# The first shift vector of a transformer block: condition standing, weights moving in rows of 512

## The chip, the cores and the metric

One NeuronCore of one Trainium2 chip runs the whole program. The metric is the device time of one execution in microseconds (us). TensorE (PE) multiplies, and its sequencer loads the standing operand (PEld); VectorE (DVE), ScalarE (ACT) and GpSimd (POOL) work on tiles of 128 partitions; SyncE (SP) issues most of the transfers. Each engine runs its own list of instructions in order, and the lists meet only at semaphores.

## What is computed

A two-layer hybrid block on 256 latent tokens and 256 context tokens, 1024 channels, float32. Each sublayer starts with an RMS norm whose result is scaled and shifted by vectors that come from a condition, one for the latent and one for the context tokens:

```
s_lat = silu(c);  s_ctx = silu(c_ctx)
mod   = s_lat @ w_ada[l] + b_ada[l]          # 9 vectors of 1024: shift, scale, gate of three sublayers
mod_c = s_ctx @ w_ada[l] + b_ada[l]
h     = rmsnorm(s, g_norm) * (1 + scale) + shift
s     = s + 0.5 * gate * (silu(h @ w_g) * (h @ w_u)) @ w_out     # the first and the last sublayer
```

The change concerns the very first shift vector (1024 channels, two conditions) of layer 0.

## The kernel before, in words

Channels lie on partitions: `x` is [128, 8, 512], eight tiles of 128 channels by 512 tokens. Every product of the large layers is made of three products of rounded halves (high and low part of the weights and of the tokens, 128x512 each, lines 1548 to 1550). Weight blocks come through a ring of four buffers (`raw`); ScalarE makes the high part (`cast`, L637) and VectorE the low part (`lower`, L1049).

The opening, by engine, in the order of each list:

- SyncE loads `ada_first` in four parts of 2 MB (L420), in the order 0, 2, 1, 3. Parts 0 and 1 are the weights of the first shift vector, parts 2 and 3 those of the first scale vector. Then it loads the first four `raw` blocks (L426).
- ScalarE issues the load of x and the small vectors, makes `c_act` = silu of the two conditions, [128, 8, 2] (L624), and `c_wide`, the same values on all partitions (L631); then the square of the last tile of x (L652). It waits for the sums of squares, takes the root (L654), casts the first two weight blocks, and waits for the first scaled tile.
- GpSimd adds up the squares of the other seven tiles (L516 to L519).
- VectorE makes the first scale vector by itself: sixteen multiply-and-sum instructions over 1024 elements (L1491), eight tiles by two conditions. Then, in `norm`, the reciprocal of the root (L1024); then `modulations`, which waits for the shift vector (`s_adad` at 8) and for its own sums and adds the biases (L995, L1001, L1011); the low parts of two blocks (L1049); and then the scaled tiles (L1033).
- TensorE, in `norm`, waits for the constants and the squares, sums them over the partitions with eight small matmuls (L1534, L1535), then runs `first_modulation`: for each of eight tiles of the shift vector, eight matmuls whose standing operand is a 128x128 block of weights and whose moving operand is the two columns of `c_act`, 64 in all, into `mod_ps` (bank 7). Behind that it waits for the reciprocal and spreads it over the partitions (L1541), and then waits for the tiles of the norm for the first two blocks (`first_two`).

So `mod_ps` gets the shift vector with channels on partitions, as VectorE reads it. All later modulation vectors are made by VectorE during the feed-forward stages and are not touched.

The tile `ada_first` lies on a part of SBUF that the hidden tiles of the first feed-forward stage (`a_hi`, `a_lo`) use later. Banks 2 and 3 of PSUM are first used by the second pair of weight blocks.

Of the kernel before, what the change touches and what calls it, by code (L numbers as in the profile page):

```python
# [9 lines left out]
ACT = mybir.ActivationFunctionType  # L10
# [3 lines left out]
P = 128  # L14
D = 1024
KD = D // P
LAT, CTX = 256, 256
TOK = LAT + CTX
# [26 lines left out]
ADA_FIRST = 2 * KD  # L45
# [66 lines left out]
def build_program(nc, a):  # L112
    with ExitStack() as ctx:
        def sb(name, shape, dt=F32, at=ctx):
            return at.enter_context(nc.sbuf_tensor(name, shape, dt))

        def sem(name):
            return ctx.enter_context(nc.semaphore(name))
# [37 lines left out]
        c_act = sb("c_act", [P, KD, 2])  # L156
# [5 lines left out]
        ident = consts[:, C_ID:C_ID + P]  # L162
# [17 lines left out]

        with ExitStack() as s:
            ada_first = sb("ada_first", [P, ADA_FIRST, KD * P], at=s)
        with ExitStack() as s:
            a_hi = sb("a_hi", [P, KF, TOK], F32R, at=s)
            a_lo = sb("a_lo", [P, KF, TOK], F32R, at=s)
# [4 lines left out]
        s = ExitStack()  # L190
# [14 lines left out]
        s = ExitStack()  # L205
# [34 lines left out]
        ps = ctx.enter_context(nc.psum_tensor("ps", [P, 8, 512], F32))  # L240
        mod_ps = ps[:, 7, 0:2 * DEPTH * ADA].rearrange("p (t s) -> p t s", s=2)
# [4 lines left out]
        s_first = [sem(f"ada_first_loaded{i}") for i in range(4)]  # L246
# [5 lines left out]
        s_out = sem("out_stored")  # L252
        s_set = sem("set_up")
        s_cact = sem("c_act_ready")
        s_adad = sem("ada_tiles_done")
        s_adv = sem("ada_first_sums")
        s_adc = sem("ada_sums_kept")
        s_mods = sem("mods_ready")
# [116 lines left out]
        def halves(n):  # L375
            return [(i, slice(i * LAT, (i + 1) * LAT)) for i in range(n // LAT)]
# [33 lines left out]
        def mods_at(l, which):  # L410

            return ((1, 3, 3), (4, 5, 5))[l][which]
# [195 lines left out]
        def _(act):  # L608
# [26 lines left out]
            def cast(j, cols=KD * P):  # L635

                return act.activation(w_hi[:, j % RING, 0:cols], raw[:, j, 0:cols], ACT.Copy)  # L637

            def landed(j, base, it=0):

                act.wait_ge(s_raw[j], 16 * (base // RING + 1) + 16 * it)

            def norm(s, l, which, n):

                def casts(lo, hi):
                    for j in range(lo, hi):
                        landed(j, STAGE_BASE[s])
                        cast(j).then_inc(s_hi, 1)
                if 0 < s < 6:
                    casts(0, 2)  # L650
                act.wait_ge(*tile_ready(s, KD - 1))
                act.activation(buf_b[:, 1, 0:n], x[:, KD - 1, 0:n], ACT.Square).then_inc(s_sq, 1)  # L652
                act.wait_ge(s_sum, s + 1)
                act.activation(rms[:, 0:n // P], ps[:, 6, 0:n // P], ACT.Sqrt, bias=eps_col[:, 0:1],  # L654
                               scale=1.0 / D).then_inc(s_rt, 1)
                if s == 0:
                    casts(0, 2)
                if which < 3:
                    act.wait_ge(s_mods, mods_at(l, which))
                for k in range(KD):  # L660
                    act.wait_ge(s_t, KD * s + k + 1)
                    if which == 3:
                        act.activation(out_t[:, k, :], buf_a[:, k % 2, 0:n], ACT.Identity,
                                       scale=nfin[:, k:k + 1]).then_inc(s_fin, 1)
                        continue
                    if k >= 2:
                        act.wait_ge(s_h, KD * s + k - 1)
                    for i, cols in halves(n):
                        last = act.activation(buf_b[:, k % 2, cols], buf_a[:, k % 2, cols], ACT.Identity,  # L669
                                              bias=mod[:, l, 3 * which * KD + k, i:i + 1],  # L670
                                              scale=gain[:, l, which, k, i:i + 1])
                    link(last)
                    act.activation(h_hi[:, k, 0:n], buf_b[:, k % 2, 0:n], ACT.Copy).then_inc(s_hhi, 1)
                    if k == KD - 3 and s in FFN_STAGE:
                        casts(2, 4)
# [301 lines left out]
        def _(vec):  # L977
# [8 lines left out]
            def modulations(l, g0, g1):  # L986

                vec.wait_ge(s_const, 48)
                t0, t1 = g0 * KD, g1 * KD
                if g0 == 0 and l == 0:  # L990
                    vec.wait_ge(s_adad, KD)
                    src = mod_ps[:, 0:KD, :]
                    t1 = KD
                    vec.wait_ge(s_adv, 2 * KD)
                    vec.tensor_tensor(  # L995
                        mod[:, 0, KD:2 * KD, :], scale_first[:, :, :],
                        vecs[:, 0, KD:2 * KD].rearrange("p (t o) -> p t o", o=1).to_broadcast([P, KD, 2]), ALU.add)
                else:
                    r0 = (ADA * l + t0 - ADA_FIRST) // 2
                    src = mod_rest[:, r0:r0 + (t1 - t0) // 2, :].rearrange("p r (t s) -> p (r t) s", s=2)  # L1000
                link(vec.tensor_tensor(  # L1001
                    mod[:, l, t0:t1, :], src,
                    vecs[:, l, t0:t1].rearrange("p (t o) -> p t o", o=1).to_broadcast([P, t1 - t0, 2]), ALU.add))
                for which in range(3):
                    if g0 <= 3 * which + 2 < g1 and which != 1:
                        gate = mod[:, l, (3 * which + 2) * KD:(3 * which + 3) * KD, :]
                        link(vec.tensor_scalar(gate, gate, 0.5, None, ALU.mult))
                    if not g0 <= 3 * which + 1 < g1:
                        continue
                    g = V_N1 + which * KD  # L1010
                    link(vec.scalar_tensor_tensor(  # L1011
                        gain[:, l, which, :, :], mod[:, l, (3 * which + 1) * KD:(3 * which + 2) * KD, :], 1.0,
                        vecs[:, l, g:g + KD].rearrange("p (t o) -> p t o", o=1).to_broadcast([P, KD, 2]),
                        ALU.add, ALU.mult))
                vec.engine_nop().then_inc(s_mods, 1)
# [492 lines left out]

        @block.tensor
        def _(pe):  # L1510
            def ada_tile(t, w):

                for k in range(KD):
                    last = pe.matmul(mod_ps[:, t, :], w[:, k * P:(k + 1) * P], c_act[:, k, :],  # L1514
                                     start=(k == 0), stop=(k == KD - 1))
                last.then_inc(s_adad, 1)

            def first_modulation():

                pe.wait_ge(s_cact, 1)  # L1520
                for t in range(KD):
                    if t % (ADA_FIRST // 4) == 0:
                        pe.wait_ge(s_first[t // (ADA_FIRST // 4)], 16)
                    ada_tile(t, ada_first[:, t, :])

            def norm(s, n):
                if s == 0:
                    pe.wait_ge(s_set, 3)
                    pe.wait_ge(s_const, 48)
                pe.wait_ge(s_acc, s + 1)  # L1530
                pe.wait_ge(s_sq, s + 1)
                for t in range(n // P):
                    cols = slice(t * P, (t + 1) * P)
                    pe.matmul(ps[:, 6, t:t + 1], buf_a[:, 0, cols], ones[:, 0:1], start=True, stop=False)  # L1534
                    ins = pe.matmul(ps[:, 6, t:t + 1], buf_b[:, 1, cols], ones[:, 0:1], start=False, stop=True)  # L1535
                ins.then_inc(s_sum, 1)
                if s == 0:
                    first_modulation()
                pe.wait_ge(s_inv, s + 1)
                for t in range(n // P):  # L1540
                    ins = pe.matmul(ps[:, 6, t * P:(t + 1) * P], inv[:, t:t + 1].to_broadcast([P, P]), ident,  # L1541
                                    start=True, stop=True)
                ins.then_inc(s_bc, 1)
# [449 lines left out]
def lay_out(v):  # L1993

    v = {k: np.asarray(z) for k, z in v.items()}

    def blocks(w):

        return w.reshape(w.shape[0] // P, P, w.shape[1] // P, P).transpose(2, 1, 0, 3).reshape(w.shape[1] // P, P, -1)
# [5 lines left out]
    tok = np.concatenate([v["x"][0], v["ctx"].reshape(CTX, D)], 0)  # L2005
    out = {"xT": tok.T.reshape(KD, P, TOK).transpose(1, 0, 2)}
    out["cT"] = np.stack([v["c"][0], v["c_ctx"]], 1).reshape(KD, P, 2).transpose(1, 0, 2)
    out["w_ada"] = blocks(v["w_ada"][0][:, :KD * P])
    out["w_ada_t"] = v["w_ada"].transpose(0, 2, 1).reshape(DEPTH * ADA, P, D)[KD:]
    out["c_rows"] = np.stack([v["c"][0], v["c_ctx"]])  # L2010
    ups, downs = [], []
# [6 lines left out]
    proj, bas, gate, merge, outs, vec, pw, rows = [], [], [], [], [], [], [], []  # L2018
    for l in range(DEPTH):
        w = v["w_in"][l]  # L2020
# [41 lines left out]
```

## Time and profile before

| | |
|---|---|
| median of 3 runs | 2533.12 us (2524.01 to 2538.27) |
| the profiled execution | 2533.53 us, span of its instructions 2531.9 us |
| TensorE matmuls busy | 2419.6 us, 96% of the span, 13688 records |
| VectorE busy | 1396.8 us, 55% |
| ScalarE busy | 869.1 us, 34% |
| GpSimd busy | 219.6 us, 9% |
| mean granted clock of TensorE | 0.973 of full speed |

Times in the trace are microseconds from the first instruction, unless marked ns. A timeline row has the start, the duration, the engine, the line of the kernel and the operation, with the tile written, the tiles read and their shapes; in brackets the idle time before it and what ended it. PE's rows overlap, since matmuls are pipelined, and so the distance between starts says what one costs. A float32 matmul appears as two records. The two levels of TensorE's clock are 1.2 and 2.4 GHz.

### The profile page before, as it was taken

What the parts mean: (1) busy time and instruction counts of PE and PEld (TensorE: products, weight loads), DVE (VectorE), ACT (ScalarE), POOL (GpSimd) and SP (SyncE); (2) the same over time, 40 slices, a digit from 0 to 9 for tenths busy, and PEclk for the clock granted to TensorE, in tenths of its full rate; (3) what the DMA queues carried; (4) which work ended last, traced back from release to release, by engine and by line L of the source; (5) the groups of instructions that cost most, each with busy time, mean ns of one, the idle gap of its engine ahead of it and who ended that gap; (6) DMA issues with size and microseconds to landing.
All of it is one profiled execution on the core that took longest, in us unless ns stands there. A gap on an engine that the chain in (4) does not pass through costs nothing.

```text
span 2531.9 us, 35964 instructions
## 1 busy us (share of the span) xinstructions
PE 2419.6 (96%) x13688; PEld 2033.6 (80%) x13688; DVE 1396.8 (55%) x2313; ACT 869.1 (34%) x1305; POOL 219.6 (9%) x284
## 2 busy tenths in 40 slices
PE   5999999999999999999999999999999999998998
PEld 5788877886578887778888778888788688978998
DVE  4788776524553436478783365553354544446554
ACT  1533312433431214243222243332335421235553
POOL 2001132000001000301111100001100001001001
PEclk9999999899999999999999999999989999989999
DMA  6455555222110105345553334433313111034555
GB/s 238 136 196 190 182 174 169 68 87 71 38 51 14 63 26 187 117 150 198 185 188 103 106 125 141 149 118 96 120 67 119 43 42 48 17 110 151 183 175 149
DMA packets 96454, 303.04 MB, mean 120 GB/s; under 512 B 10592, under 2 KB 17504, under 8 KB 95328
## 3 DMA queue, kind: packets, MB, share of 16 engines
q1 hardware_dynamic: 76912, 229.95, 27.9%
q0 software_dynamic: 18720, 69.21, 8.1%
q10 hardware_dynamic: 720, 2.44, 0.3%
q8 instruction: 73, 1.20, 0.2%
q14 instruction: 29, 0.24, 0.0%
HBM read 291.08 MB, written 10.49 MB: 119 GB/s over the span
## 4 chain that ended last, share of the span: by engine, by line
PE 88%; DVE 5%; ACT 3%; issue 2%; DMA 1%; POOL 1%; DVEq 0%; ACTq 0%; POOLq 0%; SPq 0%
PE ps L1548 23%; PE ps L1550 22%; PE ps L1549 22%; PE ps L1836 3%; PE ps L1827 3%; PE ps L1843 2%; PE ps L1726 2%; PE ps L1747 2%; DVE w_lo L1049 1%; ACT buf_b L669 1%; PE ps L1514 1%; PE ps L1881 1%; PE ps L1735 1%; PE ps L1882 1%; PE ps L1663 1%
## 5 line engine op out<-in xcount | busy, mean ns | idle before, releaser
L1548 PE MATMUL ps<-h_hi,w_hi 128*128 128x512 f32 (+1 forms) x2048 | 762.4, 372 | 36.5 <-DVE h_lo L1041 28.3
L1549 PE MATMUL ps<-h_lo,w_hi 128*128 128x512 f32 (+1 forms) x2048 | 742.5, 363 | 0.0
L1049 DVE TENSOR_TENSOR w_lo<-raw,w_hi 128x1024 fp32r<-128x1024 f32 (+2 forms) x416 | 476.2, 1149 | 482.3 <-ACT w_hi L637 477.7
L1550 PE MATMUL ps<-h_hi,w_lo 128*128 128x512 f32 (+1 forms) x2048 | 742.0, 362 | 0.0
L637 ACT ACTIVATE w_hi<-raw 128x1024 fp32r<-128x1024 f32 (+2 forms) x416 | 404.8, 974 | 673.6 <-DMA raw<-in_w_down 314.5
L1548 PEld LDWEIGHTS ps<-h_hi,w_hi 128*128 128x128 f32 x2048 | 394.4, 193 | 133.9 <-issue 62.7
L1550 PEld LDWEIGHTS ps<-h_hi,w_lo 128*128 128x128 f32 x2048 | 394.6, 193 | 58.6
L1549 PEld LDWEIGHTS ps<-h_lo,w_hi 128*128 128x128 f32 x2048 | 395.5, 193 | 54.4
L1548 PE MATMUL ps<-a_hi,w_hi 128*128 128x512 f32 (+1 forms) x960 | 345.8, 360 | 8.8 <-DVE buf_b L1471 4.5
L1550 PE MATMUL ps<-a_hi,w_lo 128*128 128x512 f32 (+1 forms) x960 | 346.1, 361 | 0.0
L1549 PE MATMUL ps<-a_lo,w_hi 128*128 128x512 f32 (+1 forms) x960 | 344.1, 358 | 0.0
L1081 DVE CUSTOM_DVE_ANT_0 ps<-ada,c_wide 128x1024 f32<-128x1024 f32 x256 | 319.3, 1247 | 6.3 <-DMA ada<-in_w_ada_t 1.0
L1548 PEld LDWEIGHTS ps<-a_hi,w_hi 128*128 128x128 f32 x960 | 180.3, 188 | 41.9 <-DVE buf_b L1471 6.6
L1549 PEld LDWEIGHTS ps<-a_lo,w_hi 128*128 128x128 f32 x960 | 180.2, 188 | 31.0
L1550 PEld LDWEIGHTS ps<-a_hi,w_lo 128*128 128x128 f32 x960 | 180.7, 188 | 29.4
L542 POOL DMA_DIRECT2D ada<-in_w_ada_t x128 | 68.3, 534 | 759.1 <-DVE ada_sum L1081 752.1
L689 ACT ACTIVATE a_hi<-buf_b 128x512 f32 (+3 forms) x88 | 50.9, 579 | 194.1 <-DVE buf_b L1067 194.1
L923 ACT ACTIVATE um<-ps 128x256 f32<-128x256 f32 x96 | 31.8, 384 | 179.1 <-PE ps L1843 179.1
L1836 PE MATMUL ps<-xm,um 128*128 128x64 f32 x768 | 89.7, 275 | 0.0
L1827 PE MATMUL ps<-tm,amT 128*128 128x64 f32 x768 | 89.2, 274 | 0.0
L1827 PEld LDWEIGHTS ps<-tm,amT 128*128 128x128 f32 x768 | 88.3, 193 | 0.3 <-ACT tm L909 0.3
L1836 PEld LDWEIGHTS ps<-xm,um 128*128 128x128 f32 x768 | 87.7, 192 | 0.0
(203 smaller groups left out, 2120.2 us busy)
## 6 DMA issues: line engine op xcount, KB each, us to landing
raw<-in_w_up SPq DMA_DIRECT2D x176, 512.0 KB, 3.9
ada<-in_w_ada_t POOLq DMA_DIRECT2D x128, 512.0 KB, 4.4
raw<-in_w_down SPq DMA_DIRECT2D x64, 384.0 KB, 3.2
raw<-in_w_gate SPq DMA_DIRECT2D x48, 512.0 KB, 3.7
raw<-in_w_down SPq DMA_DIRECT2D x64, 320.0 KB, 2.9
raw<-in_w_proj SPq DMA_DIRECT2D x32, 512.0 KB, 3.4
raw<-in_w_merge SPq DMA_DIRECT2D x16, 512.0 KB, 3.9
raw<-in_w_out SPq DMA_DIRECT2D x16, 512.0 KB, 3.5
```

The lines of the kernel that those rows point to most:

```text
L542: pool.dma_start(ada[:, j, :], a["w_ada_t"][ADA_FIRST - KD + 2 * r + j]).then_inc(s_ada[j], 16)
L637: return act.activation(w_hi[:, j % RING, 0:cols], raw[:, j, 0:cols], ACT.Copy)
L689: act.activation(a_hi[:, q, 0:n], buf_b[:, j, 0:n], ACT.Copy).then_inc(s_ahi, 1)
L1049: vec.tensor_tensor(w_lo[:, j % RING, 0:cols], raw[:, j, 0:cols], w_hi[:, j % RING, 0:cols].bitcast(F32), ALU.subtract).then_inc(s_lo, 1)
L1081: vec.tensor_tensor_reduce(ps[:, 6:8, :].rearrange("p b n -> p (b n)"), ada[:, j, :], c_wide[:, i, :], 1.0, 0.0, ALU.mult, ALU.add, ada_su ...
L1548: pe.matmul(out, wh, rows_hi[:, i, 0:n], start=first, stop=False)
L1549: pe.matmul(out, wh, rows_lo[:, i, 0:n], start=False, stop=False)
L1550: return pe.matmul(out, wl, rows_hi[:, i, 0:n], start=False, stop=last)
L1726: pe.matmul(ps[:, n % 2, keys], y[rows, 4 + t, cols], kT[rows, keys], start=True, stop=True).then_inc(sco.sem, 1)
L1747: ins = pe.matmul(ps[rows, 4 + n % 2, 0:P], v_nat[:, k, rows], probT[:, n % 2, k * P:(k + 1) * P], start=(k == k0), stop=(k == TT - 1))
L1827: ins = pe.matmul(ps[:, d, q * HD:(q + 1) * HD].rearrange("p (i c) -> p i c", c=b), amT[:, 8 * d + q, :], t, start=True, stop=True)
L1836: ins = pe.matmul(ps[:, d, q * HD:(q + 1) * HD], um[:, 8 * d + q, :], xm[:, 8 * d + q, :], start=True, stop=True)
```

## The change

The shift vector is made the other way round. The two columns of `c_act` are the standing operand and the weights move, 512 columns at a time: for each of the eight tiles of input channels two matmuls, 16 in all, into two rows of banks 2 and 3 ([2, 1024]). They run ahead of the sums of squares in TensorE's list. ScalarE copies the two rows to SBUF (`ada_rows`) after the root and ahead of its casts, and TensorE turns them with eight transposes of [2, 128] into `mod_ps`. VectorE waits for the turns in place of the eight tiles. The host lays out the weights in rows, in the same shape [8, 128, 1024].

```diff
+            ada_rows = sb("ada_rows", [P, 2, TOK], at=s)
...
                 if s == 0:
+                    act.wait_ge(s_adad, 1)
+                    act.activation(ada_rows[0:2, :, :], ps[0:2, 2:4, :], ACT.Copy).then_inc(s_adr, 1)
                     casts(0, 2)
...
                 if g0 == 0 and l == 0:
-                    vec.wait_ge(s_adad, KD)
+                    vec.wait_ge(s_adt, 1)
...
-            def ada_tile(t, w):
-
+            def first_shifts():
+
+                pe.wait_ge(s_cact, 1)
                 for k in range(KD):
-                    last = pe.matmul(mod_ps[:, t, :], w[:, k * P:(k + 1) * P], c_act[:, k, :],
-                                     start=(k == 0), stop=(k == KD - 1))
-                last.then_inc(s_adad, 1)
-
-            def first_modulation():
-
-                pe.wait_ge(s_cact, 1)
+                    if k % (ADA_FIRST // 4) == 0:
+                        pe.wait_ge(s_first[k // (ADA_FIRST // 4)], 16)
+                    for m in range(2):
+                        ins = pe.matmul(ps[0:2, 2 + m, :], c_act[:, k, :], ada_first[:, k, m * TOK:(m + 1) * TOK],
+                                        start=(k == 0), stop=(k == KD - 1))
+                ins.then_inc(s_adad, 1)
+
+            def turn_shifts():
+
+                pe.wait_ge(s_adr, 1)
                 for t in range(KD):
-                    if t % (ADA_FIRST // 4) == 0:
-                        pe.wait_ge(s_first[t // (ADA_FIRST // 4)], 16)
-                    ada_tile(t, ada_first[:, t, :])
+                    m, c = divmod(t * P, TOK)
+                    ins = pe.transpose(mod_ps[:, t, :], ada_rows[0:2, m, c:c + P], ident[0:2, 0:2])
+                ins.then_inc(s_adt, 1)
 
             def norm(s, n):
                 if s == 0:
+                    first_shifts()
                     pe.wait_ge(s_set, 3)
                     pe.wait_ge(s_const, 48)
...
                 ins.then_inc(s_sum, 1)
                 if s == 0:
-                    first_modulation()
+                    turn_shifts()
...
-    out["w_ada"] = blocks(v["w_ada"][0][:, :KD * P])
+    out["w_ada"] = v["w_ada"][0][:, :KD * P].reshape(KD, P, KD * P)
```

## Rows read from the trace of the kernel before

**Rows 1.** Chain that ended last, opening: start, duration, what.

```profile
32.94 27.32 PE ps L1514 x128
```

**Rows 2.** Waits, 0 to 66: who for whom, total, times, longest.

```profile
DVE mod L995 <- PE ps L1514: 12.7, 1, 12.7
```

**Rows 3.** Timeline of VectorE, 24 to 64.

```profile
24.34 1.70 DVE L1491 CUSTOM_DVE_ANT_0 ps<-ada_first,c_wide 128x1024 f32<-128x1024 f32 x1 [24.34 <-ACT c_wide L631]
...
46.32 1.23 DVE L1491 CUSTOM_DVE_ANT_0 ps<-ada_first,c_wide 128x1024 f32<-128x1024 f32 x1
...
47.47 0.17 DVE L1024 RECIPROCAL inv<-rms 128x4 f32<-128x4 f32 x1
60.34 0.18 DVE L995 TENSOR_TENSOR mod<-scale_first,vecs 128x16 f32<-128x16 f32 x1 [12.69 <-PE ps L1514]
...
63.12 1.28 DVE L1033 TENSOR_TENSOR buf_a<-x,ps 128x512 f32<-128x512 f32 x2
```

**Rows 4.** Stretches: length, then busy PE, PEld, DVE, ACT, POOL; PEclk, DMA share, GB/s.

```profile
32.80:60.20 27.40, 27.40 (x130) 27.40 (x130) 14.36 (x25) 2.38 (x3) 0.00 (x0) 1.00 0.25 98
...
40.00:50.00 10.00, 10.00 (x48) 10.00 (x48) 7.48 (x13) 0.00 (x0) 0.00 (x0) 1.00 0.01 2
...
80.40:300.00 219.60, 219.60 (x969) 181.83 (x970) 175.19 (x261) 79.46 (x92) 21.19 (x40) 1.00 0.55 191
```

**Rows 5.** Views of single lines: duration in ns min/median/max, first and last start.

```profile
L1514 PEld LDWEIGHTS ps<-c_act,ada_first x128: 333/333/333, 32.7 to 59.8; 128*128 128x128 f32 x128
...
L1535 PEld LDWEIGHTS ps<-ones,buf_b x48: 192/192/338, 29.7 to 2521.5; 128*128 128x128 f32 x48
```

**Rows 6.** Timeline of TensorE, first blocks, 66 to 79.

```profile
66.52 0.77 PE L1548 MATMUL ps<-h_hi,w_hi 128*128 128x512 f32 x1 [4.36 <-DVE h_lo L1041]
...
69.64 0.57 PE L1549 MATMUL ps<-h_lo,w_hi 128*128 128x512 f32 x1
70.05 0.39 PE L1550 MATMUL ps<-h_hi,w_lo 128*128 128x512 f32 x1
70.28 0.39 PE L1548 MATMUL ps<-h_hi,w_hi 128*128 128x512 f32 x1
...
78.48 0.50 PE L1548 MATMUL ps<-h_hi,w_hi 128*128 128x512 f32 x1 [1.89 <-DVE h_lo L1041]
```

**Rows 7.** Timeline of ScalarE, 20 to 64.

```profile
22.30 0.22 ACT L624 ACTIVATE c_act<-c_in 128x16 f32<-128x16 f32 x1
22.42 1.89 ACT L631 ACTIVATE c_wide<-c_wide 128x2048 f32<-128x2048 f32 x1
...
32.97 0.26 ACT L654 ACTIVATE rms<-ps,eps_col 128x4 f32<-128x4 f32 x1 [6.84 <-PE ps L1535]
...
37.21 1.06 ACT L637 ACTIVATE w_hi<-raw 128x1024 fp32r<-128x1024 f32 x1 [1.50 <-DMA raw<-in_w_up]
```

**Rows 8.** Line 420, its issues at 0.9 and at 1.9: us from issue to landing.

```profile
DMA to landing us min/median/max: 15.5/15.5/15.5
...
DMA to landing us min/median/max: 25.7/25.7/25.7
```

**Rows 9.** Timeline of TensorE, its first matmul.

```profile
29.39 0.56 PE L1534 MATMUL ps<-ones,buf_a 128*128 128x1 f32 x2 [29.39 <-POOL buf_a L519]
```

**Rows 10.** A float32 matmul of 512 columns: timeline at 618, and line 1726's view.

```profile
618.16 1.12 PE L1726 MATMUL ps<-kT,y 64*128 64x512 f32 x2
...
L1726 PE MATMUL ps<-kT,y x96: 376/589/693, 618.2 to 2010.7; 64*128 64x512 f32 x64, 64*128 64x256 f32 x32
```

**Rows 11.** Timeline of TensorE after a later norm.

```profile
1828.85 0.76 PE L1548 MATMUL ps<-h_hi,w_hi 128*128 128x512 f32 x1 [3.44 <-DVE h_lo L1041]
...
1834.84 0.39 PE L1550 MATMUL ps<-h_hi,w_lo 128*128 128x512 f32 x1
```

**Rows 12.** Groups by line and form, ScalarE: busy us, mean ns, idle before.

```profile
L909 ACT ACTIVATE tm<-ps 128x1024 f32<-128x1024 f32 x8 | 8.2, 1025 | 11.8 <-PE ps L1814 11.8
```

**Rows 13.** Timeline of VectorE in the second norm.

```profile
440.28 0.18 DVE L1024 RECIPROCAL inv<-rms 128x4 f32<-128x4 f32 x1 [1.35 <-ACT rms L654]
...
442.63 1.28 DVE L1033 TENSOR_TENSOR buf_a<-x,ps 128x512 f32<-128x512 f32 x2 [2.17 <-PE ps L1541]
```

More of the change, by code:

```diff
@@ L254, in build_program @@
         s_cact = sem("c_act_ready")
-        s_adad = sem("ada_tiles_done")
+        s_adad = sem("ada_rows_done")
+        s_adr = sem("ada_rows_taken")
+        s_adt = sem("ada_rows_turned")
         s_adv = sem("ada_first_sums")
```

## The prediction

> **What bounds the kernel now.** I read the chain of waits of the opening first. Behind GpSimd's squares and the eight small matmuls that sum them it holds 27.32 us of TensorE's L1514 in one piece, 32.94 to 60.26, and no piece near as long [rows 1]. The list of waits agrees: VectorE's L995 waits 12.7 us for L1514 and for nothing else [rows 2]. VectorE's timeline then says what else was late. Its sixteen sums of L1491 run without a pause from 24.34, and the reciprocal starts at 47.47; from then to 60.34 it stands [rows 3]. So the opening has two branches that meet at L995: TensorE, ready at 60.26, and VectorE, ready at 47.64 (47.47 + 0.17). From 80.4 to 300 TensorE is busy for the whole of the stretch, 219.60 of 219.60 us [rows 4], and the work behind it starts by its blocks, so a microsecond of the opening is a microsecond of the span.
>
> L1514 is 64 matmuls of two moving columns, which the trace has as 128 records, each with a load of 128 columns, and every load takes 333 ns [rows 5]. 27.32 / 128 = 0.213 us each. These are slow-clock loads: the same form of load at the small sums takes 0.192 us in the median and 0.338 at most [rows 5]. So in this stretch TensorE runs at its lower level, 1.2 GHz, though it has been issuing without a gap. The granted clock of that stretch reads 1.00 [rows 4], which the durations contradict, and I go by them: a 128x512 product goes from a spacing of 0.41 us to one of 0.23 at 70.05 [rows 6].
>
> **Part 1: when the wide matmuls can begin.** They need c_act, which is ready at 22.30 + 0.22 = 22.52 [rows 7], and the two halves of the shift weights, landed at 0.9 + 15.5 = 16.4 and 1.9 + 25.7 = 27.6 [rows 8]. The host's new layout has the same shape and bytes, so I leave the landings as they are. Before, TensorE is idle until 29.39 [rows 9]; now it starts at about 22.6. The second half is wanted after eight of sixteen matmuls, which take at least 6.8 us (below), to 29.4: it has landed.
>
> **Part 2: what the sixteen matmuls cost.** A float32 matmul of 512 columns is two records too: the scores' pair lasts 1.12 us, and its longer record 0.693, so the records start 0.43 apart [rows 10], about twice the float32r product of the same width at the fast clock, 0.23 [rows 6]. I take 0.85 us a matmul fast and 1.71 slow. Sixteen are 13.6 us all fast, 27.3 all slow. How many are slow is the open cost. After an idle stretch the 128x512 products run slow for 3.3 to 3.5 us (66.52 to 70.05 at the latest) [rows 6] and elsewhere for 5.9 (1828.85 to 1834.8) [rows 11]; the other boundaries between stages lie between 2.9 and 5.9. While the clock is low half the time is lost, so the sixteen take 13.6 + 1.7 = 15.3 to 13.6 + 3.0 = 16.6 us and end at 37.9 to 39.2. The bounds are 36.2 (fast from the start) and 49.9 (slow throughout). I take the middle pair, since a dense stream of 512-column work is what these matmuls are, and that is the row they resemble most; only 2 of 128 array columns hold weights, which no row shows.
> The Trainium skill (TensorE: Matmul & The Clock Gate, Part 1) says that sustained matmul activity lifts the clock to 2.4 GHz. This trace goes against it where the work is narrow: 128 records back to back stayed slow [rows 5]. By the rule the new matmuls end near 38, by the narrow row they would end at 49.9; the rivals below carry the second case.
>
> **Part 3: what follows on the path of TensorE and ScalarE.** The eight sums now stand behind the shifts: from their start at 29.39 [rows 9] to ScalarE's root at 32.97 are 3.58 us slow, 1.9 if the clock holds; the root takes 0.26 [rows 7]. Then ScalarE waits for the shifts (already done, since TensorE did them first), and copies 2 x 1024 from PSUM. The nearest row is its 128x1024 PSUM copy, 1025 ns [rows 12]; the bounds are the 16-column activation, 0.22 us, and 1.9 us, the 2048-column one [rows 7]; I take 1.03, the row of the same width. The eight turns are transposes with a 128-column load and two moving columns, the form of L1514: sixteen records at 0.213, 3.4 us slow, 1.7 fast. From the end of the wide matmuls to VectorE's L995 this is 3.58 + 0.26 + 1.03 + 3.4 and about 0.2 of handovers, 8.5 us all slow, 5.1 all fast. So the shifts are in mod_ps at 43.0 to 47.7: against VectorE's 47.64 the new branch is at or ahead of it. Queued behind the copy are ScalarE's two casts, 1.06 each, the second at 37.21 before [rows 7], now from 41 to 43 (at worst 43 to 45.4). VectorE wants them half a microsecond after L995, at 48.2, so that costs nothing. Banks 2 and 3 have no other use until the second pair of blocks.
>
> **Part 4: VectorE, the new bound.** It still has its sixteen sums to 47.6, a reciprocal, then L995, L1001, L1011 and the two L1049: 60.34 to 63.12, 2.78 us, to the first L1033 [rows 3]. New: 47.67 + 2.78 = 50.45. Spreading the inverse root on TensorE (L1541) ran beside this; it now starts behind the reciprocal. At a later norm a reciprocal at 440.28 is followed by the first L1033 at 442.63, 2.35 us, with the same eight records [rows 13]: 47.47 + 2.35 = 49.8, hidden. L1491 takes 1.23 us at 46.32 beside L1514; that wide matmuls would slow it no row of this stretch shows, and I put it at nothing. The first, 1.70, lies beside GpSimd's squares, which end by 29.4 [rows 3, 9] and do not move.
> Gain: 63.12 - 50.45 = 12.67 us, which is also the wait of L995 that goes (12.7). What is late next is VectorE's sums, so nothing that TensorE could save beyond this counts.
>
> **Part 5: does the gain survive?** Between 40 and 50 the DMA engines' share is 0.01 [rows 4]: all of the first loads have landed by then, and raw 2 and 3 are cast only in the norm, behind the new first L1033. All later loads wait for blocks or for VectorE's sums and move along. TensorE is idle before its first block as before, so the slow stretch there stays; up to 5.9 us of slow clock instead of 3.3 would be 1.3 us of delay, against the 1.89 us that TensorE waits before 78.48 [rows 6]. No cost.
> Sum against the profiled execution: its time 2533.5 with a span of 2531.9, and it lies within 0.4 us of the median, 2533.1. 2533.5 - 12.7 = 2520.8, and I add 0.2 for a copy or a turn that just misses: 2521.0.
>
> **Rivals.** *The clock stays low.* Two columns of weights might be as narrow for the clock as the two moving columns of L1514 were [rows 5]. Then the wide matmuls end at 49.9, the turns at 58.3, L995 at 58.4 and the first L1033 at 61.2: 1.9 us gained, 2531.6. For it: the whole of L1514. Against it: the 512-column products are at the fast spacing within 6 us [rows 6, 11]. 0.10.
> *Slower: loads not hidden.* Every record of L1514 has a load ahead of it that sets its pace [rows 5]. Should each of the 32 records wait for a load of 0.333 us at the slow clock, the sixteen take 27.3 + 10.7 = 38.0, end at 60.6, L995 comes at 69.1 and not at 60.34: 8.7 us lost, 2542.2. It loses from the point where one wide matmul takes more than 1.83 us ((60.34 - 8.5 - 22.6) / 16). Against it: the loads of the 128x512 products lie under the matmul before them, at a spacing that is that of the columns alone [rows 6]. 0.04.
> *It works, and something later takes it back.* The phase of the clock at later boundaries may differ between executions: slow stretches of 3.3 to 5.9 us behind a norm [rows 6, 11], and the three times of before lie 14 us apart. Half the gain gone: about 2527. 0.10.
> *The forecast.* 0.76, about 2521, its own range 2516 to 2526, a third of the 14 us by which the runs of before differ to either side.
>
> **How the numbers follow.** About 0.5% (12.7 us) is what a measurement of this kernel can tell from no change, and the forecast gain is 12.67 us, right on that line. So of the forecast's 0.76 about half, 0.38, falls on each side. Faster by over 0.5%: 0.38 and 0.04 from the give-back case by scatter, 0.42. Slower by over 0.5%: 0.04. Within 0.5%: the rest, 0.54 (the slower rival alone is at +0.35%, so it needs scatter too). The range runs from 2514, below the forecast by half the scatter of before, to 2532, which takes in the slow-clock case.
>
> **What would show it.** In the profile after: 32 records of 128x512 under the new line from about 22.6, the first few with a spacing of 0.85 and the rest of 0.43; the wait of L995 for TensorE gone or under 0.5 us; the reciprocal still at 47.5; first L1033 near 50.5 and first L1548 near 53.9; then the same picture as before, 12.7 us earlier. A TensorE spacing of 0.85 to the end would show the first rival, a reciprocal much later than 47.5 would show that the sums of squares came too late, and a slower L1491 beside the wide matmuls would be a contention that I have put at nothing.

## The result and the profile after

| | before | changed |
|---|---|---|
| median of 10 runs | 2532.32 us (2524.01 to 2538.27) | 2518.34 us (2512.54 to 2521.90) |
| ratio to before | 1 | 0.9947, 95% interval 0.993 to 0.9963 |
| span of the profiled execution | 2531.9 us | 2519.9 us |
| first scaled tile of the first norm | 63.12 | 50.45 |

The time fell by 13.4 us by the ratio (2532.32 x 0.0053), with an interval of 9.4 to 17.7; the forecast was 2521.0, a gain of 12.5. The sign of the gain is beyond doubt, whether it is more than 0.5% is not, as forecast.

All of the intended gain is in the first 50 us. VectorE's timeline of the changed kernel answers to [rows 3]; L1496 is the sums that were L1491, L1029 the reciprocal, L1000 and L1006 the two additions of biases, L1054 the low parts, L1038 the scaled tiles. The columns are start, duration, engine, line, operation.

```profile
26.04 1.89 DVE L1496 CUSTOM_DVE_ANT_0 ps<-ada_first,c_wide 128x1024 f32<-128x1024 f32 x1
...
46.24 1.23 DVE L1496 CUSTOM_DVE_ANT_0 ps<-ada_first,c_wide 128x1024 f32<-128x1024 f32 x1
47.39 0.14 DVE L1496 DVE_READ_ACCUMULATOR2_ANT scale_first<- 128x1 f32 x1
47.39 0.17 DVE L1029 RECIPROCAL inv<-rms 128x4 f32<-128x4 f32 x1
47.66 0.17 DVE L1000 TENSOR_TENSOR mod<-scale_first,vecs 128x16 f32<-128x16 f32 x1
...
48.17 2.36 DVE L1054 TENSOR_TENSOR w_lo<-raw,w_hi 128x1024 fp32r<-128x1024 f32 x2
50.45 1.28 DVE L1038 TENSOR_TENSOR buf_a<-x,ps 128x512 f32<-128x512 f32 x2
```

The bracket of 12.69 us of idle time that stood behind L995 is gone: L1000 starts 0.27 us after the reciprocal. The other branch, from TensorE's and ScalarE's timeline, answers to [rows 1, 7, 9]:

```profile
22.13 16.81 PE L1523 MATMUL ps<-ada_first,c_act 128*2 128x512 f32 x32 [22.13 <-ACT c_act L627]
38.87 0.38 PE L1544 MATMUL ps<-ones,buf_a 128*128 128x1 f32 x2
...
40.86 0.26 ACT L657 ACTIVATE rms<-ps,eps_col 128x4 f32<-128x4 f32 x1 [15.16 <-PE ps L1545]
41.02 1.00 ACT L661 ACTIVATE ada_rows<-ps 2x1024 f32<-2x1024 f32 x1
41.92 1.99 ACT L640 ACTIVATE w_hi<-raw 128x1024 fp32r<-128x1024 f32 x2
42.07 1.01 PE L1532 MATMUL ps<-consts,ada_rows 2*128 2x2 f32 x8 [1.25 <-ACT ada_rows L661]
```

The turned shifts are there at 43.08, 4.6 us ahead of VectorE's L1000. The chain of work that ended last says the same: from 23.91 to 47.5 it consists of the sixteen L1496 one after another, with no piece of TensorE among them. Two of them (start, duration, what):

```profile
30.22 1.23 DVE ps L1496
31.54 1.24 DVE ps L1496
```

What came of the gain behind the opening? The reciprocals of the later norms are good milestones. Before, the second norm's is at 440.28 [rows 13], and two later ones are:

```profile
1823.62 0.18 DVE L1024 RECIPROCAL inv<-rms 128x4 f32<-128x4 f32 x1 [0.79 <-ACT rms L654]
...
2319.55 0.16 DVE L1024 RECIPROCAL inv<-rms 128x2 f32<-128x2 f32 x1
```

In the changed kernel the three are:

```profile
430.44 0.18 DVE L1029 RECIPROCAL inv<-rms 128x4 f32<-128x4 f32 x1 [0.79 <-ACT rms L657]
1814.13 0.18 DVE L1029 RECIPROCAL inv<-rms 128x4 f32<-128x4 f32 x1 [1.01 <-ACT rms L657]
2307.82 0.16 DVE L1029 RECIPROCAL inv<-rms 128x2 f32<-128x2 f32 x1
```

The lead is 12.67 us at the first scaled tile, 9.8 at 430, 9.5 at 1814, 11.7 at 2308 and 12.0 at the end. 2.8 us go in the first feed-forward stage, where TensorE waited for a low part longer than before, and the granted clock was low for a while behind that wait. The row of the changed kernel, and the row of before at the same block:

```profile
316.87 0.50 PE L1558 MATMUL ps<-a_hi,w_hi 128*128 128x512 f32 x1 [2.74 <-DVE w_lo L1054]
```

```profile
327.68 0.51 PE L1548 MATMUL ps<-a_hi,w_hi 128*128 128x512 f32 x1 [0.86 <-DVE w_lo L1049]
```

So the lead is 10.8 us here and was 12.7 at the block before. Over 300 to 340 the stretch view has the length, PE's busy time, its records, PEclk, DMA share and GB/s, first changed, then before (the same stretch of time, not the same work, since the changed kernel is some 11 us ahead):

```profile
300.00:340.00 40.00, 36.64 (x150) 0.96 0.49 156
```

```profile
300.00:340.00 40.00, 38.52 (x166) 1.00 0.60 195
```

It is no fixed price of the change: another execution of the changed kernel waits 1.35 us at that place and reaches its second norm at 427.64, 12.6 us ahead of before, with nothing lost.

### The profile page after: what moved, and what is told of

Its sections match the earlier page's. It is cut to its first block, busy times and chain, and to the rows that moved or that the text cites. A ratio compares the mean times of both kernels' runs of the same rounds, so it can differ in the third digit from the quotient of the medians.

```text
span 2519.9 us, 35789 instructions
## 1 busy us (share of the span) xinstructions
PE 2408.4 (96%) x13600; PEld 2008.4 (80%) x13600; DVE 1398.4 (55%) x2313; ACT 870.1 (35%) x1306; POOL 218.5 (9%) x284
## 4 chain that ended last, share of the span: by engine, by line
PE 87%; DVE 6%; ACT 3%; DMA 2%; issue 2%; ACTq 0%; SPq 0%; DVEq 0%
PE ps L1558 23%; PE ps L1560 22%; PE ps L1559 22%; PE ps L1846 3%; PE ps L1837 3%; PE ps L1853 2%; PE ps L1736 2%; PE ps L1757 2%; DVE w_lo L1054 1%; ACT buf_b L674 1%; PE ps L1891 1%; PE ps L1745 1%; PE ps L1892 1%; DVE ps L1496 1%; PE ps L1673 1%
## 5 line engine op out<-in xcount | busy, mean ns | idle before, releaser
L1558 PE MATMUL ps<-h_hi,w_hi 128*128 128x512 f32 (+1 forms) x2048 | 761.7, 372 | 35.8 <-DVE h_lo L1046 27.3
L1054 DVE TENSOR_TENSOR w_lo<-raw,w_hi 128x1024 fp32r<-128x1024 f32 (+2 forms) x416 | 477.4, 1152 | 479.6 <-ACT w_hi L640 475.4
L1558 PE MATMUL ps<-a_hi,w_hi 128*128 128x512 f32 (+1 forms) x960 | 347.7, 362 | 10.8 <-DVE buf_b L1476 4.5
L1559 PEld LDWEIGHTS ps<-a_lo,w_hi 128*128 128x128 f32 x960 | 182.6, 190 | 30.7
L1060 DVE SCALAR_TENSOR_TENSOR x<-ps,mod,x 128x256 f32 (+1 forms) x80 | 35.7, 480 | 98.6 <-PE ps L1560 98.6
```

What stands on the lines that cost most here:

```text
L1054: vec.tensor_tensor(w_lo[:, j % RING, 0:cols], raw[:, j, 0:cols], w_hi[:, j % RING, 0:cols].bitcast(F32), ALU.subtract).then_inc(s_lo, 1)
L1558: pe.matmul(out, wh, rows_hi[:, i, 0:n], start=first, stop=False)
L1559: pe.matmul(out, wh, rows_lo[:, i, 0:n], start=False, stop=False)
```

## The experiments

The question is which of two things brings the gain, the width of the moving rows or the place ahead of the sums; whether VectorE's sums are what bounds now; how much TensorE has in hand; and what raises the clock. All the runs are read by one number above all, the start of the first scaled tile (L1033 or its successor). Two executions of the changed kernel have it at 50.45 and 50.57, while their spans lie 10.5 us apart.

| kernel | last shift matmul done | first addition of biases | first scaled tile | ratio to before (95%) |
|---|---|---|---|---|
| before | 60.26 | 60.34 | 63.12 | |
| narrow_ahead | 49.8 | 53.68 | 56.79 | 0.9963 (0.9944 to 0.9982) |
| wide_behind_sums | 49.2 | 51.06 | 53.85 | 0.9955 (0.9934 to 0.9976) |
| changed | 38.9 | 47.66 | 50.45 | 0.9947 (0.993 to 0.9963) |
| changed_again | 39.2 | 47.78 | 50.57 | 0.994 (0.9918 to 0.9962) |
| eight_more | 45.2 | 49.09 | 51.88 | a single run: 2509.8 us |
| rows_of_128 | 44.6 | 48.84 | 51.63 | a single run: 2522.0 us |
| half_sums | 38.6 | 42.87 | 45.66 | 0.9903 (0.9872 to 0.9934) |
| early_silu | 34.6 | 46.73 | 49.52 | 0.9933 (0.991 to 0.9955) |
| split_scale | 35.8 | 43.48 | 46.27 | 0.9939 (0.9917 to 0.9962) |

**The order alone.** The edit, on the kernel before:

```diff
             def norm(s, n):
                 if s == 0:
+                    first_modulation()
                     pe.wait_ge(s_set, 3)
...
-                if s == 0:
-                    first_modulation()
```

> The kernel before with its 64 narrow matmuls moved ahead of the sums of squares: the order alone, without the width. Theory: they run 22.1 to 49.5 at the slow clock, 0.213 us a record, then the sums 3.6 us to 53.1, the root, the reciprocal; first addition of biases 53.7, first scaled tile at 56.5, 6.6 us ahead of before and 6.0 us behind the changed kernel (ratio to before 0.9974). Rival, in which an early start lets the clock rise for narrow matmuls too: records of 0.107 us after some 6 us, ends near 39, first scaled tile 50.5.

The narrow matmuls took as long as in [rows 1], only earlier:

```profile
22.36 27.46 PE L1514 MATMUL ps<-c_act,ada_first 128*128 128x2 f32 x128 [22.36 <-ACT c_act L624]
...
53.57 0.18 DVE L1024 RECIPROCAL inv<-rms 128x4 f32<-128x4 f32 x1 [6.06 <-ACT rms L654]
```

The first scaled tile is 6.3 us ahead of before. The root, now behind everything on TensorE, is what VectorE waits for. An early start does not raise the clock for them, so the rival falls.

**The width alone.** The edit, on the changed kernel:

```diff
                 if s == 0:
-                    first_shifts()
                     pe.wait_ge(s_set, 3)
...
                 if s == 0:
+                    first_shifts()
                     turn_shifts()
```

> The changed kernel with the wide matmuls back behind the sums of squares: the width alone, without the order. If both parts of the change count (theory): sums 29.3 to 32.7, wide matmuls 32.7 to about 49.5 (16.8 us, as they took in the changed kernel), copy 1.0, turns 1.0, VectorE's first addition of biases at about 52.0 and the first scaled tile at 54.8, against 63.12 before and 50.45 changed. Gain over before 8.3 us (ratio 0.9967). If the gain is the order's (rival), the first scaled tile is near 63; if it is all the width's, it is at 50.5.

9.3 us ahead of before, where 8.3 was expected: the wide matmuls took 16.36 us, and the turns 0.65 where I had set 1.0. So both parts count, 6.3 and 9.3 each by itself, 12.7 together and not 15.6: the pair is cut off by VectorE. With that bound out of the way (half_sums, next) the pair is 17.5 ahead of before, which is more than 15.6. Most of that surplus, 1.6 us, is in the eight small sums: behind the wide matmuls they take 1.95 us, and 3.55 before, where they run at the slow clock.

**Is VectorE the new bound?** Eight of its sums left out:

```diff
-                    vec.wait_ge(s_adv, 2 * KD)
+                    vec.wait_ge(s_adv, 1 + KD)
...
+            vec.memset(scale_first[:, :, 1:2], 0.0).then_inc(s_adv, 1)
...
-                for i in range(2):
+                for i in range(1):
                     if t or i:
-                        vec.wait_ge(s_adv, 2 * t + i)
+                        vec.wait_ge(s_adv, 1 + t)
```

> The changed kernel without the eight sums of the second condition (that half of the first scale vector is left at zero, so its output is not the reference's). Theory, VectorE's sums are the new bound and TensorE's branch is ready at 43.1: VectorE is done near 36.5, waits for the turns, first addition of biases 43.2, first scaled tile 46.0, 4.4 us ahead of the changed kernel, time about 2514. Rival, something else ends with the sums at 47.6 (TensorE, a transfer, the casts): first scaled tile stays at 50.4.

45.66: a gain of 4.8 us on top. VectorE now stands for TensorE's branch again: 3.0 us for the root, whose sums lie behind the wide matmuls, and then for the turns, as this row of VectorE's waits (who for whom, total, times, longest) shows:

```profile
DVE mod L1000 <- PE ps L1533: 1.8, 1, 1.8
```

(Its sums ended at 37.8 and not near 36.5, since it stood 1.15 us for the fourth quarter of the weights, which landed at 32.6; that cost nothing here.) The rival, in which something else ends at 47.6, falls. 4.8 us is TensorE's slack measured from the other side, against 4.6 read from the profile (its wide matmuls ended 0.3 sooner here).

**How much has TensorE in hand?** The first eight wide matmuls done twice:

```diff
             def first_shifts():
 
                 pe.wait_ge(s_cact, 1)
+                for k in range(4):
+                    if k == 0:
+                        pe.wait_ge(s_first[0], 16)
+                    for m in range(2):
+                        pe.matmul(ps[0:2, 2 + m, :], c_act[:, k, :], ada_first[:, k, m * TOK:(m + 1) * TOK],
+                                  start=(k == 0), stop=(k == 3))
```

> The changed kernel with the first eight wide matmuls done twice, 6.8 us more of TensorE at the fast clock. Theory, TensorE's branch has 4.5 us in hand (43.1 against 47.6): wide matmuls end at 45.8, turns at 50.0, first scaled tile 52.8, only 2.4 us later than changed. If there were no slack it would be 57.3; if the extra work is hidden altogether, 50.5.

51.88, so 6.8 us more work cost 1.4. It is 0.9 less than expected, since here the clock was fast sooner: from the first of the extra matmuls to the first of the others are 8.77 us (22.55 to 31.32), 1.9 over the 6.86 of sixteen records at the fast spacing, so some 3.9 us ran slow, against 5.9 in the changed kernel. And the turns took 0.65, at the fast clock:

```profile
48.35 0.65 PE L1538 MATMUL ps<-consts,ada_rows 2*128 2x2 f32 x8 [1.25 <-ACT ada_rows L661]
```

**What raises the clock, and what a row costs.** The same weights in rows of 128, tile by tile:

```diff
-                for k in range(KD):
-                    if k % (ADA_FIRST // 4) == 0:
-                        pe.wait_ge(s_first[k // (ADA_FIRST // 4)], 16)
-                    for m in range(2):
-                        ins = pe.matmul(ps[0:2, 2 + m, :], c_act[:, k, :], ada_first[:, k, m * TOK:(m + 1) * TOK],
+                pe.wait_ge(s_first[0], 16)
+                pe.wait_ge(s_first[1], 16)
+                for m in range(KD):
+                    for k in range(KD):
+                        ins = pe.matmul(ps[0:2, 2 + m // 4, (m % 4) * P:(m % 4 + 1) * P], c_act[:, k, :],
+                                        ada_first[:, k, m * P:(m + 1) * P],
```

> The changed kernel with its weights moved in rows of 128 and not 512, tile by tile: 64 matmuls, 128 records of 128 columns, all behind the landing of the second half of the weights at 27.6. If only the columns that stream count: 128 records at 0.107 us fast plus some 3 us for the slow start, 27.6 to 44.3, first scaled tile 51.3, 0.9 us behind changed. If each record costs as much as the narrow ones did (0.213), or the clock stays low, they end at 54.9 and the first scaled tile is at 62.

```profile
27.62 16.99 PE L1523 MATMUL ps<-ada_first,c_act 128*2 128x128 f32 x128 [27.62 <-DMA ada_first<-in_w_ada]
```

128 records in 16.99 us beside 32 records in 16.8: what streams is what costs, 8192 columns in both, and four times the instructions cost nothing. L1514 has 128 records too, each with two moving columns behind a load of 128, and takes 27.4 us. The whole of that difference is the clock. At the slow level a record is 0.213 us from the next here as in L1514, 27.3 us for 128 of them, and a wide one 0.853, 27.3 us for 32. At the fast level they are 0.110 apart here and 0.429 in the wide form, 14.0 and 13.7 us. L1514 never ran fast; the form nearest to it, the small sums of the changed kernel (a load of 128, one moving column), has 0.112 there, which would be 14.3. So at one clock both ways round cost nearly the same, and neither rows of 512 nor fewer instructions are part of the gain. The gain of the width, 27.4 to 16.8 us, is that the clock rises where the weights move and did not where they stood. The first scaled tile, 51.63, is 1.2 us behind changed because this run's matmuls began 5.5 us later.

**Can VectorE start earlier?** ScalarE makes both forms of the condition as soon as the condition has landed:

```diff
+            act.activation(c_act[:, :, :], c_in[:, :, :], ACT.Silu).then_inc(s_cact, 1)
+
+            def wide(f):
+
+                act.wait_ge(s_wide, 16 * (f + 1))
+                act.activation(c_wide[:, :, :], c_wide[:, :, :], ACT.Silu).then_inc(s_wact, 1)
+
+            wide(0)
             act.wait_ge(s_const, 32)
             act.dma_start(consts[:, :], a["consts"][:, 0:N_KEEP]).then_inc(s_const, 16)
-            act.activation(c_act[:, :, :], c_in[:, :, :], ACT.Silu).then_inc(s_cact, 1)
             act.wait_ge(s_gain, 16)
             act.wait_ge(s_set, 3)
...
-            wide(0)
```

> The changed kernel with only the earlier condition: ScalarE makes both forms before it waits for the small vectors. Theory (VectorE bounds): its sums start when their weights land, 22.0 and not 23.9; three to four of them then lie beside GpSimd's squares at about 2.0 us each in place of three, so they end near 45.9 and not 47.5, and the first scaled tile is at 48.8, 1.6 us ahead of changed. TensorE is ready by about 39 and has 7 us in hand. Rival (TensorE still bounds): the whole 5.6 us of its earlier start show, first scaled tile near 45.

49.52, 0.9 us ahead of changed and not 1.6. TensorE was ready 8 us before VectorE, which excludes the rival. VectorE's sums did start at 22.03, but five of them, not three, now took 1.46 to 2.11 us: GpSimd's squares slowed down in their turn and lasted to 30.7 instead of 29.0, so the two kept each other busy for longer.

```profile
22.48 1.90 POOL L521 TENSOR_TENSOR buf_a<-x 128x512 f32<-128x512 f32 x1
24.45 2.12 POOL L522 TENSOR_TENSOR buf_a<-buf_a 128x512 f32<-128x512 f32 x1
26.65 1.90 POOL L521 TENSOR_TENSOR buf_a<-x 128x512 f32<-128x512 f32 x1
```

**Sharing the scale vector.** On top of that edit, two of the eight scale tiles go to TensorE, between the halves of the wide matmuls; VectorE makes twelve sums:

```diff
-            for t in range(KD):
+            for t in range(2, KD):
...
+                def scales():
+                    pe.wait_ge(s_first[2], 16)
+                    for k in range(KD):
+                        pe.matmul(ps[0:2, 1, 2 * P:4 * P], c_act[:, k, :],
+                                  ada_first[:, KD + k // 4, (k % 4) * 2 * P:(k % 4 + 1) * 2 * P],
+                                  start=(k == 0), stop=(k == KD - 1))
+
                 for k in range(KD):
+                    if k == KD // 2:
+                        scales()
...
```

> The changed kernel with two more edits. ScalarE makes the two forms of the condition before it waits for the small vectors, so that TensorE can begin when the first quarter of the weights lands, near 16.5. And two of the eight tiles of the first scale vector go the way of the shift: eight matmuls of 256 columns between the halves of the wide ones, ten turns in place of eight; VectorE makes 12 sums and not 16. Theory: wide 16.5 to 26.2, 256-column ones to 29.6, wide to 36.4, sums 38.2, copy 39.9, turns 41.3; VectorE done near 40.3; first scaled tile 44.2, 6.2 us ahead of the changed kernel's 50.45, ratio to before about 0.9925. Rival: VectorE's sums start no earlier than before and run slower beside GpSimd's squares, or the casts come too late: first scaled tile 46 or later.

46.27, 4.2 us ahead of changed, where 6.2 were expected. That is within the rival's number (46 or later), but not for its reasons alone: the sums did start earlier, at 22.32, and the casts were done by 40.9; three of the sums were slow beside GpSimd's squares. I had left out a landing: after four sums VectorE has used up the third quarter of the weights and stands for the fourth, which lands at 32.7. The profile of half_sums shows the same landing at 32.6.

```profile
27.89 1.89 DVE L1496 CUSTOM_DVE_ANT_0 ps<-ada_first,c_wide 128x1024 f32<-128x1024 f32 x1
...
32.77 1.23 DVE L1496 CUSTOM_DVE_ANT_0 ps<-ada_first,c_wide 128x1024 f32<-128x1024 f32 x1 [2.94 <-DMA ada_first<-in_w_scale]
```

The opening is shorter in both, but their whole times are not shown to beat the changed kernel's: on the same chip the ratios to before are 0.9933, 0.9939 and 0.994 (changed_again), each with an interval of 0.2% either way, 5 us, that swallows 0.9 and 4.2 us.

**The changed kernel again**, for the scatter.

> The changed kernel itself, beside the others on the same chip: first scaled tile 50.4 and a ratio to before of about 0.995. What differs between its executions behind the opening is the scatter against which the others are read.

Its first scaled tile is that of the first profile within 0.12 us, its span 2509.4 and not 2519.9. Of the 10.5 us, 2.8 are the place in the first feed-forward stage told above, and 7.5 sit in the second mixer stage: the kernel before had 495.9 us from 1823.62 to 2319.55, where these two have 493.7 and 486.2. Set record beside record of TensorE, the first execution gains 1.3 us on the second in this stage until its 2221.5, and then loses 8.8 by 2288.9. The loss begins with one stretch of 123 records, a mixture of small float32 matmuls and of the 128x256 products of rounded halves. In the stretch view (length, PE busy, records, PEclk, DMA share, GB/s), first the execution of 2519.9, then that of 2509.4:

```profile
2221.50:2243.90 22.40, 22.40 (x123) 0.59 0.20 59
```

```profile
2219.90:2236.40 16.50, 15.91 (x123) 0.91 0.27 80
```

The same work takes 5.9 us more at a granted clock of 0.59 than at 0.91. The profile of before has the same matmuls at the low clock too, so this is no effect of the change:

```profile
2236.00:2258.50 22.50, 22.50 (x124) 0.59 0.21 59
```

What decides the clock of this place in an execution is open, and so is how much of the 10 to 14 us by which whole runs of one kernel differ comes from it. That the clock has a part in them fits the ten runs of the changed kernel: the two quickest, 2512.5 and 2515.3 us, have the highest mean granted clocks, 0.973 and 0.972, and the other eight 0.968 to 0.971.

## Why the prediction was right, point by point

*The bound, and its successor.* TensorE's branch was the later one by 12.7 us and VectorE's sums were next: half_sums shows it from the one side and eight_more from the other. The gain of the opening is the idle time of one row [rows 3]. That it came out at 12.67 us to the hundredth is luck: changed_again has 12.55. So is the nearness of 13.4 us to 12.5 over whole runs, where the interval is 9.4 to 17.7.

*The wide matmuls.* Begin 22.13 (said 22.6), end 38.9 (said 37.9 to 39.2). They took 16.8 us, a little over the 15.3 to 16.6 that were said, and end inside the range because they began sooner. The fast spacing of a record is 0.43 and the slow one 0.85, as put together from [rows 10]; seven records ran slow, to 28.05, 5.9 us, the long end of [rows 11]. The loads of two columns are short and hidden:

```profile
27.21 0.13 PEld L1523 LDWEIGHTS ps<-ada_first,c_act 128*2 128x2 f32 x1 [0.72 <-issue]
28.05 0.09 PEld L1523 LDWEIGHTS ps<-ada_first,c_act 128*2 128x2 f32 x1 [0.71 <-issue]
28.48 0.09 PEld L1523 LDWEIGHTS ps<-ada_first,c_act 128*2 128x2 f32 x1 [0.34 <-issue]
```

So the first two rivals fall: the clock did rise with two of 128 array columns in use, and no record waits for its load. By the rule of the Trainium skill (TensorE: Matmul & The Clock Gate, Part 1), sustained matmuls raise the clock; it holds for moving rows of 512 and of 128, and narrow_ahead shows a second time that it does not hold for two moving columns, 27.46 us long.

*The copy.* Said 1.03, measured 1.00; a PSUM copy of 1024 columns costs the same on 2 partitions as on 128 [rows 12].

*The turns: a term that was mis-sized.* I took sixteen records at 0.213 slow, 3.4 us, or 1.7 fast, the form of L1514. They are eight records, one each: a turn is 0.107 us from the next at the slow clock, a quarter of the 0.426 that I took (1.01 us in all, with the end of the last one), and 0.062 at the fast one (0.65 in eight_more). The Trainium skill (TensorE: Matmul & The Clock Gate, Terms) gives float32 loads and matmuls in transpose mode as four times faster; these rows agree, and the page would have set the term right. It lay on the branch with slack, so the forecast did not feel it. The eight small sums before them took 1.95 us, the fast end of what was said (1.9 to 3.58).

*The hidden parts.* The casts end at 43.9, before 48.2; the spread of the inverse root, 47.62 to 49.7, ends before 50.45; L1496 takes 1.23 us beside the wide matmuls as beside the narrow ones. All three at nothing, as said.

*Whether the gain survives.* It did on the whole. The slow stretch at the first block did get longer, from 3.5 us (66.52 to 70.05) to some 5 (53.85 to 58.95), and cost nothing, as Part 5 said: TensorE's wait behind the first pair of blocks shrank from 1.89 us to 1.25, and the next block starts at 65.81, 12.67 ahead of 78.48. The give-back rival, put at 0.10, describes the profiled execution in its middle (9.5 us left of 12.7 at 1814), but it is scatter: in the later part 2.5 us come back, and ten runs have 13.4. Why TensorE waits longer at the start of the down products in one execution than in another (2.74, 1.35 us) is left open; no run was made for it. The chains of work that ended last differ there in a transfer: 4.30 us of `raw<-in_w_down` from 310.80 in the one, 5.61 us of `ada<-in_w_ada_t` from 306.11 in the other.

## What to carry to other kernels

Ask of a matrix-vector product which operand should stand: with the vector standing, the cost is the columns that move; with the weights standing, it is a full load for each block. In float32 and at one clock the two came to nearly the same here, and what told was the clock, which rose for the one and stayed at half for the other. Moving the work ahead of a wait brought 6.3 us without any of that. Before such a change, read what the other branch into the same wait has in hand, since that and not the time saved (here 17.2 us of TensorE's branch, 60.3 to 43.1) is the gain. A profile of one execution places the opening to a tenth of a microsecond, while whole runs of this kernel differ by 10: test a change of the opening by its milestones.

## What the runs showed of the hardware that was not expected

- TensorE at 1.2 GHz through 27 us of back-to-back matmuls with two moving columns (0.213 us a record, in two kernels), but at 2.4 GHz 3.4 to 5.9 us after the start of a stream of 512 columns (3.4 in early_silu, about 3.9 in eight_more, 5.9 in changed), with only two array columns in use. The granted clock read 1.00 in that slow stretch; the durations tell.
- At one clock 64 float32 matmuls with a load of 128 columns and two moving ones cost what 16 with two standing and 512 moving columns do: 128 x 0.213 and 32 x 0.853, both 27.3 us at the slow level.
- A float32 transpose of [2, 128] is one record of 0.11 us at the slow and 0.06 at the fast clock, where a plain float32 matmul with a 128-column load is two of 0.213 and 0.107.
- VectorE's 1024-element sum takes 1.23 us alone or beside TensorE and 1.89 to 2.11 beside GpSimd's squares, which go from 1.04 and 1.26 to 1.90 and 2.12 themselves. In the rows of the changed kernel each slowed one ends about 1.1 us behind the end of the other engine's (26.83 and 27.93, 29.03 and 30.12), as if the two took turns. Starting the sums earlier lengthens both: three slowed sums became five.
